# The final norm of the first block's output: its sum of squares, root and scaling moved along the groups of the next feed-forward

## The reference, cut to what matters

```python
def first_block(...):
    ...
        x = x + g2 * expert_choice_moe(h2, w_router[l], w_gate[l], w_up[l], w_down[l])
    ...
    return rms_norm(x, final_g)          # x / sqrt(mean(x*x) + eps) * final_g

def second_block(x, c, ...):
    cond = jax.nn.silu(c)
    for l in range(DEPTH_2):             # 2 layers
        mod = cond @ w_ada[l] + b_ada[l]
        sh1, sc1, g1, sh2, sc2, g2, sh3, sc3, g3 = jnp.split(mod, N_MOD, axis=-1)
        h = modulate_2(rms_norm_2(x), sh1, sc1)
        x = x + 0.5 * g1[:, None, :] * swiglu(h, w_ff1_in[l], w_ff1_out[l])
        ...
def swiglu(h, w_in, w_out):              # hidden width 2816
    gate, up = jnp.split(h @ w_in, 2, axis=-1)
    return (jax.nn.silu(gate) * up) @ w_out
```

## Time and profile before

| what | us |
| --- | --- |
| median of 3 runs | 2613.94 |
| lowest and highest run | 2610.3, 2615.94 |
| the profiled execution | 2608.99 |
| its span, first to last instruction | 2607.2 |
| TensorE busy | 2224.5 (85%) |
| VectorE busy | 1062.7 (41%) |
| ScalarE busy | 478.9 (18%) |
| mean granted TensorE clock | 0.927 |

### The profile page before, as it was taken

One profiled execution on the slowest core, in us unless ns is written; L12 is line 12 of the kernel. 1 busy time (PEld: TensorE's weight loads), 2 busy tenths in 40 slices (PEclk: granted clock), 3 DMA queues, 4 the chain that ended last, 5 costly groups with the idle time before them and its releaser, 6 DMA issues. The chain is left out here.

```text
span 2607.2 us, 29754 instructions
## 1 busy us (share of the span) xinstructions
PE 2224.5 (85%) x11904; PEld 1528.4 (59%) x11904; DVE 1062.7 (41%) x1875; ACT 478.9 (18%) x1059; POOL 6.1 (0%) x11
## 2 busy tenths in 40 slices
PE   8999887666665666666899999999999999999998
PEld 5786732111111111111688886888888888778887
DVE  5753631000001000000686457567238645756531
ACT  3203110000000000000222144322112203442220
POOL 0000000000000000000000000000000000000000
PEclk9999988878778888877999999999999999999999
DMA  9653789999999999999977431086447763105430
GB/s 392 231 210 144 302 352 419 427 427 429 427 428 428 428 428 428 428 428 427 415 289 302 175 122 65 2 341 269 170 154 310 291 248 114 47 28 237 167 129 17
DMA packets 75201, 721.65 MB, mean 277 GB/s; under 512 B 8656, under 2 KB 11728, under 8 KB 13520
## 3 DMA queue, kind: packets, MB, share of 16 engines
q1 hardware_dynamic: 75088, 720.09, 67.4%
HBM read 719.01 MB, written 1.05 MB: 276 GB/s over the span
## 5 line engine op out<-in xcount | busy, mean ns | idle before, releaser
L1287 PE MATMUL bank<-pool,moe_x_cur 128*32 128x512 f32 x1776 | 270.7, 746 | 140.7 <-DMA pool<-in_w_expert 140.7
L1775 PE MATMUL bank<-trunk_proj,pool 128*128 128x256 f32 x1408 | 309.1, 380 | 0.0
L1775 PEld LDWEIGHTS bank<-trunk_proj,pool 128*128 128x128 f32 x1408 | 265.5, 190 | 37.5 <-issue 2.5
L1287 PEld LDWEIGHTS bank<-pool,moe_x_cur 128*32 128x32 f32 x1776 | 54.7, 123 | 343.3 <-DMA pool<-in_w_expert 234.9
L1312 PE MATMUL bank<-pool,moe_hidT 128*32 128x512 f32 x864 | 146.9, 819 | 71.0 <-DMA pool<-in_w_expert 64.2
L1473 DVE TENSOR_TENSOR moe_hid<-bank,moe_silu 128x512 f32<-128x512 f32 x16 | 11.1, 691 | 447.7 <-ACT moe_silu L1429 447.7
L1853 PE MATMUL bank<-pool 128*128 128x256 f32 x640 | 152.1, 381 | 0.0
L2159 PE MATMUL bank<-pool 128*128 128x256 f32 x672 | 148.1, 380 | 0.0
L1853 PE MATMUL bank<-spare,trunk_mix 128*128 128x256 f32 x640 | 146.5, 382 | 1.7 <-ACT first_layer_sq L1912 1.7
L1853 PE MATMUL bank<-pool,trunk_mix 128*128 128x256 f32 x640 | 144.7, 379 | 0.0
L2159 PEld LDWEIGHTS bank<-pool 128*128 128x128 f32 x672 | 127.3, 190 | 19.9 <-issue 2.6
(11 more groups left out here) (648 smaller groups left out, 2940.0 us busy)
## 6 DMA issues: line engine op xcount, KB each, us to landing
pool<-in_w_expert SPq DMA_DIRECT2D x165, 2048.0 KB, 35.6
pool<-in_w_ff SPq DMA_DIRECT2D x132, 1024.0 KB, 6.9
pool<-in_w_ada SPq DMA_DIRECT2D x66, 1024.0 KB, 9.0
moe_more<-in_w_expert SPq DMA_DIRECT2D x23, 2048.0 KB, 35.8
pool<-in_w_in SPq DMA_DIRECT2D x40, 1024.0 KB, 5.0
pool<-in_w_mod SPq DMA_DIRECT2D x24, 1024.0 KB, 8.0
pool<-in_w_out SPq DMA_DIRECT2D x10, 1024.0 KB, 9.9
pool<-in_small SPq DMA_DIRECT2D x2, 2560.0 KB, 9.1
```

Source lines behind the costliest of these rows:

```text
L1287: mm = pe.matmul(ps[b][quarter[g], :], x_cur[:, u], w[:, b, g], start=u == 0, stop=u == up_panels - 1)
L1775: mm = pe.matmul(self.ps[3 + q % 2][:, 0:T], w, x[:, k], start=k == 0, stop=k == nk - 1)
```

## The change

The fold moves from behind the four halves to behind the gate of pair 1 (ahead of side panel 1); the column sum from group 0 to group 1, behind its first product; the root from ahead of group 0 to group 1, behind its four copies; the reciprocal and the first four scalings from ahead of group 0 to behind group 2, and the other four scalings to behind group 4. "First, second, third, fifth" group are groups 0, 1, 2 and 4 in the code. The squares stay.

```diff
-    def act_group(self, sc, g):
+    def act_group(self, sc, g, beside=None):
         x, y, z = (b[:, 0:T] for b in self.banks(g))
         for n, (bank, at, done) in enumerate(((x, 0, 1), (z, 3, 2), (x, 1, 3), (x, 2, 5))):
             sc.wait_ge(self.product, 7 * (self.n + g) + done)
             if g and n == 0:
                 sc.wait_ge(self.joined, 5 * (self.n + g) - 2)
             sc.activation(self.a[at], bank, ACT.Copy).then_inc(self.taken, 1)
+        if beside:
+            beside(sc)
         if g:
             self.act_out(sc, g - 1)
...
             for g in range(GROUPS):
-                groups.pe_group(pe, g, x_sum if g == 0 and not early else None)
+                groups.pe_group(pe, g, x_sum if g == 1 and not early else None)
...
+        def x_root(sc):
+            sc.wait_ge(x_summed, 1)
+            sc.activation(d.root, ps[5][:, 0:T], ACT.Sqrt, bias=c["eps"][:, 0:1], scale=1.0 / D).then_inc(x_rooted, 1)
+
+        def x_fold(ve):
+            ve.wait_ge(x_squared, KD)
+            for half in (4, 2, 1):
+                ve.tensor_tensor(x_sq[:, 0:half], x_sq[:, 0:half], x_sq[:, half:2 * half], ADD)\
+                    .then_inc(x_folded, 1 if half > 1 else 2)
+                ve.wait_ge(x_folded, {4: 1, 2: 2, 1: 4}[half])
+
+        def x_scale(ve, tiles):
+            for k in tiles:
+                ve.scalar_tensor_tensor(xT[:, k], xT[:, k], final_g[:, k:k + 1], d.rstd, MUL, MUL)
...
-                if p == 1 and not early:
-                    sc.wait_ge(x_summed, 1)
-                    sc.activation(d.root, ps[5][:, 0:T], ACT.Sqrt, bias=c["eps"][:, 0:1], scale=1.0 / D)\
-                        .then_inc(x_rooted, 1)
             for g in range(GROUPS):
-                groups.act_group(sc, g)
+                groups.act_group(sc, g, x_root if g == 1 and not early else None)
...
                 if p == 0:
                     groups.dve_halves(ve)
-                if p == 0 and not early:
-                    ve.wait_ge(x_squared, KD)
-                    for half in (4, 2, 1):
-                        ve.tensor_tensor(x_sq[:, 0:half], x_sq[:, 0:half], x_sq[:, half:2 * half], ADD)\
-                            .then_inc(x_folded, 1 if half > 1 else 2)
-                        ve.wait_ge(x_folded, {4: 1, 2: 2, 1: 4}[half])
+                if p == 1 and not early:
+                    x_fold(ve)
                 for n in beside_pair[p]:
                     side_panel(ve, early + n)
             for g in range(GROUPS):
-                if g == 0 and not early:
+                groups.dve_group(ve, g, [side(n) for n in beside_group[g]])
+                if g == 2 and not early:
                     ve.wait_ge(x_rooted, 1)
                     link(ve.reciprocal(d.rstd, d.root))
-                    for k in range(KD):
-                        ve.scalar_tensor_tensor(xT[:, k], xT[:, k], final_g[:, k:k + 1], d.rstd, MUL, MUL)
-                groups.dve_group(ve, g, [side(n) for n in beside_group[g]])
+                    x_scale(ve, range(0, 4))
+                if g == 4 and not early:
+                    x_scale(ve, range(4, KD))
                 if g in turn_behind:
                     tile_add(ve, n_early + turn_behind[g])
```

## The result

Ten runs of each kernel: the changed kernel took 2605.97 us (2603.66 to 2609.64), the kernel before 2610.22 us (2606.55 to 2615.94; the three runs that the prediction started from are among these ten, and two of them are its slowest). The ratio is 0.9984, 95% interval 0.9976 to 0.9992, so between 2.1 and 6.3 us faster. The measured 4.25 us are still less than the 5.2 us that the prediction called telling from no change, so its case "the same" (0.82) held. The profiled execution took 2608.16 us, with a span of 2606.4.

A forecast was written before the change was run, and what follows sets the result against it. VectorE's queue was taken to bind until group 1's third product on TensorE. 2.6 us won net, less 1.2 for a slow clock, gave -1.4 us: 2612.5 us against the three-run median 2613.94, range 2608.3 to 2616.5.

The forecast's parts named there:

- the same: Whole kernel: the time would change by less than the 5.2 us that runs can tell from no change; chance 0.82.
- What bounds: Second block's feed-forward: VectorE's queue binds until TensorE's wait in group 1 ends at 1297.61 us.
- items 1 to 3: Groups 0 and 1: 4.96 us leave VectorE's queue, side panel 0's landing limits the net to 2.6; TensorE's wait grows to 3.8.
- the signs: Listed marks of a right forecast, among them VectorE idle 2.2 us before side panel 0 and group 2 beginning at about 1305.3.
- Item 4: TensorE behind group 1's wait: a slow stretch at half clock costs 1.2 us, between 0 and 1.6.
- rival C: Behind group 1's wait: over 6 us at half clock costs 3.4, with 2.6 won, so 0.8 us slower; chance 0.10.
- A: Behind group 1's wait: no slow stretch, or one inside the wait, so 2.6 us faster, 2611.3 us; chance 0.16.
- Items 5 to 7: Root's table loads on ScalarE, scalings behind groups 2 and 4, and load queue: each fits in idle time, cost 0.
- the rule on the drain: ScalarE, group 1: a skill's rule adds about 1380 ns per table load, shrinking the gain by 0.9 us; the prediction doubted it.
- item 7: Load queue on SyncE: its waits shift, but what is behind them is needed a group or more later; cost 0.

The follow-up runs named there:

- fold_back: The changed kernel with the fold put back behind the four halves, ahead of side panel 0; 2602.99 us, ratio 0.9965 to the kernel before.
- panel_early: The changed kernel with the load of feed-forward panel 10 issued behind side panels 0 and 1 instead of ahead of them; ratio 0.9974 to the kernel before.
- scale_only: The kernel before with only the reciprocal and the scaling moved, behind groups 2 and 4; ratio 0.9980 to the kernel before.
- after_look: The changed kernel with nothing altered, profiled a third time; one run, group 2 began 42.1 us after the block's first matmul.
- after_again: The changed kernel once more, nothing altered; ratio 0.9989 to the kernel before.
- before_again: The kernel before once more, nothing altered; ratio 0.9994 to the kernel before.
- fold_back_side2: The changed kernel with the fold back behind the halves and side panel 2 moved behind group 0's joins; 2602.07 us, ratio 0.9967 to the kernel before.
- before_look: The kernel before with nothing altered, profiled a third time; one run, group 2 began 42.0 us after the block's first matmul.
- no_x_norm: The changed kernel without the reciprocal and the eight scalings of x; ratio 0.9986 to the kernel before.
- more_tables: The changed kernel with one more pair of ScalarE table switches ahead of the root in group 1; ratio 0.9992 to the kernel before.
- long_wait_2: The changed kernel with side panel 3 moved ahead of group 0's joins, second run of that kernel; group 2 began at 44.8 us from the block's first matmul.

## Why the prediction was right or wrong

**What bounds, and items 1 to 3: right.** Gross 4.96 us, 2.3 us given back to the landing, net 2.6: the join moved by 2.6, the new DMA wait is 2.30 us (forecast 2.3, and 2.2 among the signs), TensorE's wait 3.65 (3.8). fold_back, panel_early and scale_only show the two sizes apart.

**Item 4, the clock: the term was mis-sized.** It put 1.2 us on every execution, behind a wait of 3.8. Measured, it is 0 in the first profile of the changed kernel (wait 3.65 us) and 2.7 us in the third (3.63); in the second the wait was only 1.87, and nothing followed it. So of the prediction's signs the half clock right behind the wait did not come in the first profile, and group 2 began at 1264.80 + 39.4 = 1304.2 on the time axis of before, where the sign said 1305.3. The ends I gave, 0 and 1.6, were also too narrow: I took a whole slow stretch to be the one behind the first wait of before, while the rows of 1615 already showed one of over 6 us and I kept that for rival C. C's price (3.4, less 2.6) was nearly met by after_look: all of the gain gone. A and C were two outcomes of one kernel, not two theories of it, and the forecast between them is a time that no profile showed.

**Items 5 to 7: right.** The root's two loads cost nothing with about 2 us of room left, and the scaling nothing behind groups 2 and 4; the rule on the drain did not hold. No engine waited for a load in the rest of the ten groups (item 7).

**How the numbers follow: the step that put the time out of the range.** The forecast was 1.4 us taken from 2613.94, the median of three runs. Ten runs of the same kernel gave 2610.22, 3.7 us less; the profiled execution, 2608.99, had pointed down and I added 5 us to it. Of the 6.5 us between 2612.5 and 2605.97 that step is 3.7, the clock term 1.2, and 1.6 remain. The interval of the difference, 2.1 to 6.3 us, holds the 2.6 that the groups show, and so does after_again's, 0.5 to 5.2. before_again, no change at all, came out 0.8 us below before by the medians, with an interval that holds 1. Where the remaining 1.6 us come from stays open: fold_back, panel_early, scale_only and fold_back_side2 also came out 2 to 4 us faster than their groups. The profiles show no gain behind the groups, as said above; what is left is the expert stage, whose length varies in any kernel, and executions that were not profiled.

## What to carry to other kernels

Before work is moved off a spot where it "costs", ask what lands or arrives while it runs: here a fold of 2.5 us hid a load's landing so exactly that the trace of before had no wait to show, and moving it gave half of the gain back. Waits of the engine that looks busiest are not the gain when another engine's queue sets when the last of them ends: add up that queue, and a wait that vanishes comes back further on. A median of three runs is no anchor for an effect of 0.1% (here it lay 3.7 us above that of ten); compare profiles from a point just ahead of the change.

## What the runs showed of the hardware

What a TensorE wait of 3.6 us costs is a matter of chance, as far as these profiles show: the same wait in the same kernel was followed by no slow stretch or by 6.8 us at 1.2 GHz (2.7 us lost). Shorter waits can be followed by one too: the 2.55 us before the column sum were, by 3.4 us at half clock (1.6 to 1.7 us lost), in before, before_look and scale_only, and not in before_again. The 1.80 to 1.90 us ahead of the block's first matmul were in four of the fourteen profiles (after_again, no_x_norm, more_tables, long_wait_2), where the clock fell 0.8 to 1.1 us into the lead pair. Waits of 1.28 to 1.87 us in group 1 never were, in seven profiles; so the length of a wait alone doesn't settle it.

Loads queued one behind the other landed at an even pace: side panels 0 and 1, issued 0.4 us apart, landed 2.5 us apart, so taking one load of 1 MB out from ahead of side panel 0 brought its landing 2.5 us forward (12.3 us after its issue in panel_early, 14.8 in the changed kernel). A switch of ScalarE's tables took 1.28 us, with the next activation 0.02 us behind it, three times in a row in more_tables.
